# Slot lists of a mixture-of-experts layer: from a one-hot product on TensorE to a table in DRAM

## The chip, the cores and the metric

The kernel runs on one core of one Trainium2 chip. The metric is device time in microseconds (us) of one launch. The engines are TensorE (PE), VectorE (DVE), ScalarE (ACT), GpSimd (POOL) and SyncE (SP); each has its own queue of instructions, and they meet only at semaphores. DMAs are issued from the queues of SP, ACT and POOL.

## The reference, cut to what matters

The program is two transformer blocks on 512 tokens of width 1024. The first block ends in a hierarchical mixture of experts: each token chooses one of 4 groups and in it 2 of 8 experts, so there are 1024 pairs of token and expert over 32 experts.

```
g_sel = argmax(g_logits); top_vals, top_idx = top_k(e_in, 2)
weights = g_w[:, None] * softmax(top_vals)
eid = (g_sel[:, None] * 8 + top_idx).reshape(-1)
# sort the pairs by expert, pad each expert's list, run each block of rows through its expert
hid = silu(xb @ w_gate[e]) * (xb @ w_up[e]);  y = hid @ w_down[e]
y = sum(y_buf[dest].reshape(T, 2, D) * weights[..., None], axis=1)
```

Everything else (a mixer of mLSTM and differential attention ahead of it; a second block with pooling, windowed attention and a 4096 wide feed-forward behind it) is not touched by the change.

## The kernel before, in words

**Stages.** The first mixer runs first, then the routing, then a loop over the 32 experts, then the second block. All weights come through `ring`, six slots of 2 MB, filled by SP. The loop of an expert uses three of them (gate, up, down).

**The routing.** DVE computes the two one-hot choices of each token. A product on TensorE ("rank") counts, for each pair, how many earlier pairs go to the same expert. From it DVE writes `tab` (the number of the first block of each expert, and how many extra blocks it has) and `dest`: for each of the two choices k of each token the slot it gets, counting in blocks of 64 slots. 57 blocks are held.

**The slot lists.** The loop needs the inverse: for each block the list of the 64 tokens in it (`ids[:, block, 0]`) and the 64 rows of the results (`ids[:, block, 1]`, which is token + 512 k). An empty slot holds 1024, which is out of bounds, so that its row is skipped. Before the change DVE splits `dest` into position and block (`slot_at`), makes one-hot tables of both (`POS1H`, `BLK1H`), multiplies one with the row number minus 1024 (`BLKV`), and eight accumulating matmuls on PE ("slots", L600) bring each row number to its place; five small DVE instructions turn that into `idx[:, 0]` (the list of block 0) and `ids`. All of this is on the chip.

**The loop.** For each block POOL copies a column of `ids` to `idx` (`pick`, L1063), gathers 64 rows of `h_rows` from DRAM with an indirect DMA (`gather_rows`, L1067) and scatters the results of the block before with another (`scatter_results`, L1073). PE transposes the rows (`turn_rows`, L608), ACT and DVE split them into a high and a low part (XTS, L1284 and L1737), and PE multiplies (gate and up at L619, down at L646 and L653). The weights are split too: ACT writes the high half (`weights_hi`, L1280), DVE the rest (`weights_lo`, L1732), each in two halves for each of the three units (0 gate, 1 up, 2 down). While expert e runs, ACT and DVE split the weights of e + 1.

**What sets the order.** Nothing is planned: each engine runs its instructions in the order in which they are written. SP loads the weights of experts 0 and 1 as slots of the first stage come free. The load of expert e + 2 waits until the product that reads the raw weights of expert e is done (`freed`, L950, and the DMA at L957).

**Ahead of the loop.** POOL waits for `h_out` (the rows are in DRAM) and `tab_ready`, then for `idx_kept[0]`, and issues the gather of block 0. ACT splits the weights of expert 0; for unit 2 it waits for the "slots" product, since `HI[2]` lies over the routing tables. DVE runs `weights_lo` of unit 0, then `rows_lo(0)`, then units 1 and 2.

Of the kernel before, what the change touches and what calls it, by code (L numbers as in the profile page):

```python
# [26 lines left out]
P = 128  # L27
# [20 lines left out]
BLOCKS_HELD = BLOCKS_MAX + PER_EXPERT_MAX + 1  # L48
NO_ROW = 2 * T
# [13 lines left out]
N_CONSTS2 = 24  # L63
N_SMALL = 17
N_CONSTS = 15
# [28 lines left out]
def build(nc, A, out):  # L94
# [8 lines left out]
    with ctx:  # L103
# [33 lines left out]
        slot_at = sb("slot_at", [P, 2, 2, TT], I32)  # L137
# [29 lines left out]
        IOS, ROWV = m(10112, BLK).bitcast(I32), m(10176, 2 * TT)  # L167
        POS1H, BLK1H, BLKV = m(10240, 2 * TT, BLK), m(10752, 2 * TT, BLOCKS_HELD), m(11264, 2 * TT, BLOCKS_HELD)
        ROWF, HALF2 = m(15360, BLOCKS_HELD)[0:BLK], m(15424, BLOCKS_HELD)[0:BLK]
# [89 lines left out]
        slots_hot = sem("slots_hot")  # L259
        idx_kept = [sem(f"idx_kept{k}") for k in range(2)]  # L260
        waits_met = sem("waits_met")
        ids_ready = sem("ids_ready")
# [22 lines left out]
        consts2 = sem("consts2")  # L285
        pool_step = sem("pool_step")
# [119 lines left out]
        def _(pe):  # L406
# [451 lines left out]
        def _(sp):  # L858
# [73 lines left out]
            sp.dma_start(sink[:, :], A["attn_sinks_2"].to_broadcast([P, W2_HEADS])).then_inc(sink_in, 16)  # L932

# [44 lines left out]
        def _(pool):  # L978
# [9 lines left out]
            def select(t, pattern, base, mult, op, fill, wait=False):  # L988
# [12 lines left out]
            const(pool.iota(inv16[:, :], [[1, 16]], base=1, channel_multiplier=0,  # L1001
                            allow_small_or_imprecise_dtypes=True), True)
# [7 lines left out]
            def roots(names, width):  # L1010
                for nm in names:
# [24 lines left out]
            pool.iota(IOS, [[1, BLK]], base=0, channel_multiplier=0).then_inc(consts2, 1)  # L1036
            pool.iota(ROWV, [[P, 2 * TT]], base=-NO_ROW, channel_multiplier=1,
                      allow_small_or_imprecise_dtypes=True).then_inc(consts2, 1)
            pool.memset(SUM2, 0.0).then_inc(consts2, 1)
            pool.wait_ge(consts2, 10)  # L1040
            for k in range(-1, 2):
                pool.affine_select(out=SUM2, in_=SUM2, pattern=[[-1, 2 * BLK]], base=k * BLK, channel_multiplier=1,
                                   compare_op=ALU.not_equal, fill=1.0).then_inc(consts2, 1)
                pool.wait_ge(consts2, 12 + k)
# [5 lines left out]
            pool.wait_ge(consts2, 14 + W2_HEADS)  # L1050
            pool.affine_select(out=BM, in_=BM, pattern=[[0, W2_HEADS], [-1, 2 * P]], base=P, channel_multiplier=1,
                               compare_op=ALU.is_ge, fill=NEG).then_inc(consts2, 1)
            pool.wait_ge(consts2, 15 + W2_HEADS)
# [3 lines left out]

            pool.wait_ge(h_out, 16 * TT)
# [31 lines left out]

            pool.wait_ge(idx_kept[0], 1)
            gather_rows()
            pool.wait_ge(ids_ready, 1)
# [37 lines left out]
        def _(act):  # L1131
# [47 lines left out]
            act.wait_ge(row_dve, 2)  # L1179
            act.activation(REM, RM, ACT.Exp, scale=-1.0).then_inc(row_act, 1)  # L1180
# [228 lines left out]
        def _(vec):  # L1409
# [251 lines left out]
            vec.wait_ge(consts2, 14)  # L1661
# [52 lines left out]
            step(vec.tensor_scalar(slot_at[:, 1, :, :], dest[:, :, :], BLK.bit_length() - 1, None, ALU.logical_shift_right))  # L1714
            pos, blk = (slot_at[:, a, :, :].rearrange("p k t -> p (k t)").unsqueeze(2) for a in range(2))
            step(vec.tensor_tensor(POS1H, over(pos, 2 * TT, BLK), over(IOS.unsqueeze(1), 2 * TT, BLK), ALU.is_equal))
            step(vec.tensor_tensor(BLK1H, over(blk, 2 * TT, BLOCKS_HELD),
                                   over(IOS[:, 0:BLOCKS_HELD].unsqueeze(1), 2 * TT, BLOCKS_HELD), ALU.is_equal))
            vec.tensor_tensor(BLKV, BLK1H, over(ROWV.unsqueeze(2), 2 * TT, BLOCKS_HELD), ALU.mult).then_inc(slots_hot, 1)
            leave(vec.tensor_scalar(ROWF, filled(vec, "slots")[0:BLK, 0:BLOCKS_HELD], float(NO_ROW), None, ALU.add), "slots")  # L1720
            left(vec, "slots")
            step(vec.tensor_scalar(HALF2, ROWF, float(T), -float(T), ALU.is_ge, ALU.mult))
            vec.tensor_tensor(idx[:, 0, :], ROWF[:, 0:1], HALF2[:, 0:1], ALU.add).then_inc(idx_kept[0], 1)
            step(vec.tensor_copy(ids[:, :, 1], ROWF))
            vec.tensor_tensor(ids[:, :, 0], ROWF, HALF2, ALU.add).then_inc(ids_ready, 1)
# [30 lines left out]
            for half_ in range(2):  # L1756
                weights_lo(0, 0, 0, half_)
            rows_lo(0)
            for u in range(1, 3):
                for half_ in range(2):  # L1760
                    weights_lo(0, u, 0, half_)
            each_expert(vec, block_vec)
# [149 lines left out]
```

## Time and profile before

| What | Value |
|---|---|
| median of 3 runs | 1673.29 us (1669.67 to 1675.77) |
| the profiled execution's own time | 1673.29 us |
| its span, first to last instruction | 1671.3 us |
| PE busy | 1488.6 us (89%) |
| DVE busy | 924.7 us (55%) |
| ACT busy | 733.1 us (44%) |
| POOL busy | 243.7 us (15%) |
| mean granted TensorE clock | 0.910 |

A share of busy time is a mean over stages. The routing and the first blocks of the loop lie at about 400 to 470 us of the span, the loop of the experts at about 438 to 990 us. Times within the span count from its start. PEld is the weight load of TensorE. "issue" is time in which an engine waited for nothing that the profile shows. An engine's name with a q (POOLq, SPq) is its queue: the issuing of a DMA or a register instruction. For a DMA issued from POOL the trace has an instruction (DMA_INDIRECT) whose duration is POOL's own part in it; the data land later.

### The profile page before, as it was taken

The page shows a single profiled execution, that of the slowest core. Times are in us where ns is not written, and L with a number is a line of the kernel's source. Part 1 is how long each engine was busy: PE and PEld are TensorE (multiplying, and loading weights), DVE is VectorE, ACT ScalarE, POOL GpSimd, SP SyncE. Part 2 cuts the span into 40 slices and gives each one's busy share as a digit, 9 for nine tenths or more (in the row PEclk, how much of TensorE's full clock was granted, in tenths as well). Part 3 has the DMA queues.
Part 4 walks back from the last instruction along what each step waited for, and adds up shares of the span by engine and source line. Part 5 has one row for each costly group of instructions (what it writes and reads, how often), then busy time and mean ns, then how long its engine had stood idle before and what let it go on. Part 6 is the DMA issues. An engine that isn't in the chain of part 4 may idle for free.

```text
span 1671.3 us, 19199 instructions
## 1 busy us (share of the span) xinstructions
PE 1488.6 (89%) x6529; PEld 1084.4 (65%) x6530; DVE 924.7 (55%) x1050; ACT 733.1 (44%) x847; POOL 243.7 (15%) x247
## 2 busy tenths in 40 slices
PE   7899988788499999999999968989699999969968
PEld 6788754435367676767676754544388788858746
DVE  6833144413688898889888852462644224421543
ACT  4333232201388888888888841341123213321120
POOL 1011000013222322232222210140000000000030
PEclk8999867788599999999999988979799999979979
DMA  5222420033199999999999986200012222222201
GB/s 203 67 85 101 165 87 1 0 93 126 53 366 385 387 387 387 388 387 385 386 383 382 379 270 181 100 4 23 0 51 101 101 101 101 101 101 96 80 7 44
DMA packets 135235, 294.35 MB, mean 176 GB/s; under 512 B 17870, under 2 KB 19980, under 8 KB 135180
## 3 DMA queue, kind: packets, MB, share of 16 engines
q1 hardware_dynamic: 122732, 270.61, 44.7%
q10 hardware_dynamic: 7168, 14.59, 2.4%
q0 software_dynamic: 5280, 8.40, 1.6%
q8 instruction: 37, 0.61, 0.2%
q14 instruction: 18, 0.15, 0.0%
HBM read 289.64 MB, written 12.85 MB: 181 GB/s over the span
## 4 chain that ended last, share of the span: by engine, by line
PE 64%; DVE 15%; issue 9%; ACT 5%; DMA 4%; DVEq 2%; POOL 1%; SPq 0%; ACTq 0%; POOLq 0%
PE ps L794 11%; PE ps L815 10%; PE ps L457 7%; DVE ring_r L1732 7%; PE ps L619 5%; PE ps L569 3%; PE ps L768 3%; PE ps L653 3%; PE ps L847 3%; PE ps L646 2%; DMA ring<-in_w_gate 2%; PE ps L412 2%; ACT hi L1280 2%; PE ps L501 2%; PE ps L675 2%
## 5 line engine op out<-in xcount | busy, mean ns | idle before, releaser
L1732 DVE TENSOR_TENSOR ring_r<-ring,hi 128x2048 fp32r<-128x2048 f32 x192 | 427.0, 2286 | 45.5 <-ACT hi L1280 45.5
L1280 ACT ACTIVATE hi<-ring 128x2048 fp32r<-128x2048 f32 x192 | 356.5, 1908 | 4.8 <-PE ps L600 2.5
L1459 DVE TENSOR_TENSOR ring_r<-ring,ring_r 128x4096 fp32r<-128x4096 f32 x25 | 110.6, 4425 | 173.8 <-ACT ring_r L1151 173.8
L815 PE MATMUL ps<-ring_r,ats 128*128 128x512 f32 x768 | 179.0, 396 | 4.0 <-DVE ats L1862 3.2
L815 PEld LDWEIGHTS ps<-ring_r,ats 128*128 128x128 f32 x768 | 147.2, 192 | 35.9 <-issue 4.8
L1151 ACT ACTIVATE ring_r<-ring 128x4096 fp32r<-128x4096 f32 x25 | 90.5, 3620 | 167.2 <-PE ps L815 133.7
L1014 POOL TENSOR_TENSOR rsv<-msv,half 128x1 f32<-128x1 f32 (+2 forms) x32 | 32.8, 1027 | 839.1 <-DVE msv L1419 839.1
L619 PE MATMUL ps<-ring_r,XTS 128*128 128x512 f32 x512 | 129.4, 395 | 1.8 <-DVE XTS L1737 1.8
L619 PE MATMUL ps<-hi,XTS 128*128 128x512 f32 x512 | 127.5, 391 | 0.0
L653 PE MATMUL ps<-hi,HIDS 128*64 128x512 f32 x512 | 126.4, 400 | 0.0
L794 PE MATMUL ps<-ring_r,ring_r 128*128 128x512 f32 x512 | 123.1, 393 | 1.8 <-DVE hi L1850 1.8
L457 PE MATMUL ps<-ring_r,ring_r 128*128 128x512 f32 x448 | 111.3, 402 | 5.2 <-DVE M L1484 4.5
L619 PEld LDWEIGHTS ps<-ring_r,XTS 128*128 128x128 f32 x512 | 97.1, 190 | 25.2 <-issue 2.0
L794 PEld LDWEIGHTS ps<-ring_r,ring_r 128*128 128x128 f32 x512 | 97.3, 190 | 22.6 <-issue 2.2
L619 PEld LDWEIGHTS ps<-hi,XTS 128*128 128x128 f32 x512 | 96.9, 189 | 20.4
L653 PEld LDWEIGHTS ps<-hi,HIDS 128*64 128x64 f32 x512 | 71.5, 140 | 53.1 <-issue 7.4
L457 PEld LDWEIGHTS ps<-ring_r,ring_r 128*128 128x128 f32 x448 | 85.9, 194 | 23.8 <-DVE M L1484 4.9
L646 PE MATMUL ps<-ring_r,HIDS 128*64 128x512 f32 x256 | 79.1, 461 | 22.3 <-ACT HIDS L1299 22.3
L1073 POOL DMA_INDIRECT results<-M,idx x33 | 54.5, 1651 | 133.2 <-ACT M L1308 132.9
L1067 POOL DMA_INDIRECT M<-h_rows,idx x33 | 66.0, 1999 | 49.2 <-POOL idx L1063 27.3
L646 PEld LDWEIGHTS ps<-ring_r,HIDS 128*64 128x64 f32 x256 | 36.9, 154 | 49.7 <-issue 36.1
L1063 POOL COPY idx<-M 64x1 int32 x64 | 34.3, 537 | 237.2 <-DMA results<-M,idx 166.7
(295 smaller groups left out, 1943.9 us busy)
## 6 DMA issues: line engine op xcount, KB each, us to landing
ring<-in_w_gate SPq DMA_DIRECT2D x32, 2048.0 KB, 14.2
ring<-in_w_up SPq DMA_DIRECT2D x32, 2048.0 KB
ring<-in_w_down SPq DMA_DIRECT2D x32, 2048.0 KB, 14.7
ring<-in_w_ff SPq DMA_DIRECT2D x16, 2048.0 KB, 8.0
ring<-in_w_in SPq DMA_DIRECT2D x8, 2048.0 KB, 8.4
X<-in_x ACTq DMA_DIRECT2D x8, 512.0 KB, 5.2
ring<-in_w_out SPq DMA_DIRECT2D x2, 2048.0 KB
M<-results ACTq DMA_DIRECT2D x8, 512.0 KB, 7.4
```

Of the source, the lines that this page charges most:

```text
L457: ins = pe.matmul(o, a, b, start=(i == 0 and k == 0), stop=(i == 2 and k == DT - 1))
L619: ins = pe.matmul(ps[:, u, :], XTS[:, k, :, :].rearrange("p s b -> p (s b)"), w[:, k, :], start=(part == 1 and k == 0), stop=(part == 0 an ...
L646: ins = pe.matmul(ps[0:BLK, 4 + c, :], HIDS[:, 0, f, :], w_rest[:, f, c * 512:(c + 1) * 512], start=(f == 0), stop=False)
L653: ins = pe.matmul(ps[0:BLK, 4 + c, :], HIDS[:, a, f, :], w_top[:, f, c * 512:(c + 1) * 512], start=False, stop=(a == 1 and f == FT - 1))
L794: ins = pe.matmul(o, w[a][:, k, f * P:(f + 1) * P], HTS[b][:, k, :], start=(i == 0 and k == 0), stop=(i == 2 and k == DT - 1))
L815: ins = pe.matmul(ps[:, 2 * t + c, :], ATS[a][:, 4 * (n % 4) + k, t * P:(t + 1) * P], w[b][:, k, c * 512:(c + 1) * 512], start=(n % 4 == 0 ...
L1067: pool.indirect_dma_start(out=XG, out_offset=None, in_=h_rows, in_offset=bass.IndirectOffsetOnAxis(idx[:, 0, 0:1], 0), bounds_check=T - 1, ...
L1073: pool.indirect_dma_start(out=results, out_offset=bass.IndirectOffsetOnAxis(idx[:, 1, 0:1], 0), in_=YB.rearrange("p c n -> p (c n)"), in_o ...
L1151: act.activation(split_hi[j % 2][:, :], ring[:, s, :], ACT.Copy).then_inc(s_hi, 1)
L1280: act.activation(HI[u][:, c], ring[:, s, c], ACT.Copy).then_inc(w_hi, 1)
L1459: vec.tensor_tensor(ring_r[s][:, :], ring[:, s, :], split_hi[j % 2][:, :].bitcast(F32), ALU.subtract).then_inc(s_lo, 1)
L1732: vec.tensor_tensor(ring_r[s][:, c], ring[:, s, c], HI[u][:, c].bitcast(F32), ALU.subtract).then_inc(w_lo, 1)
```

## The change

The slot lists are made through a table in DRAM, `slot_tokens` (57 x 64 slots of two 32-bit numbers). POOL fills a tile (`unheld`) with 1024 at the program's start, and SP writes it to the table, between its small loads and its first load of weights. Two iotas for each choice k write `tokid`: the token, and token + 512 k. When `dest` is ready, POOL issues eight indirect DMAs (one for each k and tile of 128 tokens), each of which scatters 128 entries of 8 bytes to the slots named in `dest`, waits for all of them, loads the whole table back into `ids` with a plain DMA of its own queue, waits for that, picks the list of block 0, and gathers. The "slots" product and the ten DVE instructions around it go. ACT's wait for "slots" becomes one for `dest_ready`. DVE splits the weights of units 0 and 1 ahead of `rows_lo(0)` instead of unit 0 alone.

```
+        slot_tokens = nc.dram_tensor("slot_tokens", [SLOTS, 2], I32, kind="Internal").ap()
-            pe.wait_ge(slots_hot, 1)
-            o = open_turn(pe, "slots", 7)
-            for j in range(2 * TT):
-                ins = pe.matmul(o[0:BLK, 0:BLOCKS_HELD], POS1H[:, j, :], BLKV[:, j, :], start=(j == 0), stop=(j == 2 * TT - 1))
-            fill_turn(ins, "slots")
...
+            sp.wait_ge(consts, N_CONSTS)
+            sp.dma_start(slot_tokens.rearrange("(p n) o -> p (n o)", p=BLK),
+                          unheld[:, :, :].rearrange("p n o -> p (n o)")).then_inc(table_in, 16)
...
+            const(pool.memset(unheld[:, :, :], NO_ROW))
+            for k in range(2):
+                const(pool.iota(tokid[:, k, :, 0], [[P, TT]], base=0, channel_multiplier=1))
+                const(pool.iota(tokid[:, k, :, 1], [[P, TT]], base=k * T, channel_multiplier=1), k == 1)
...
+            pool.wait_ge(table_in, 16)
+            pool.wait_ge(dest_ready, 1)
+            for k in range(2):
+                for t in range(TT):
+                    pool.indirect_dma_start(
+                        out=slot_tokens, out_offset=bass.IndirectOffsetOnAxis(dest[:, k, t:t + 1], 0),
+                        in_=tokid[:, k, t, :], in_offset=None).then_inc(ids_out, 16)
+            pool.wait_ge(ids_out, 16 * 2 * TT)
             pool.wait_ge(h_out, 16 * TT)
             pool.wait_ge(tab_ready, 1)
...
+            pool.dma_start(ids, slot_tokens.rearrange("(n p) o -> p n o", p=BLK)).then_inc(idx_in, 16)
+            pool.wait_ge(idx_in, 16)
+            pick(0, 0)
             pool.wait_ge(idx_kept[0], 1)
             gather_rows()
-            pool.wait_ge(ids_ready, 1)
...
                 if u == 2:
-                    filled(act, "slots")
+                    act.wait_ge(dest_ready, 1)
...
-            step(vec.tensor_copy(dest[:, :, :], RS[:, 6:8, :]))
-            step(vec.tensor_scalar(slot_at[:, 0, :, :], dest[:, :, :], BLK - 1, None, ALU.bitwise_and))
...
+            vec.tensor_copy(dest[:, :, :], RS[:, 6:8, :]).then_inc(dest_ready, 1)
```

POOL's queue at the end of the routing, before the change: L1054 is the last of the tables for the second block, L1067 the gather of block 0, and behind it the loop begins.

```order
L1049 TENSOR_SCALAR M<-M 128x256 x8
L1051 AFFINE_SELECT M<-M 128x2048 [waits consts2]
L1054 AFFINE_SELECT M<-M 128x2048 [waits consts2]
L1067 DMA M<-h_rows,idx 64x1024 [waits idx_kept0,tab_ready,h_out]
L379 UNCONDITIONAL_BRANCH [waits ids_ready]
```

The same place of the changed kernel (its line numbers are its own: L1063 the scatter into the table, L1100 the load of the table, L1072 the pick, L1076 the gather).

```order
L1050 TENSOR_SCALAR M<-M 128x256 x8
L1052 AFFINE_SELECT M<-M 128x2048 [waits consts2]
L1055 AFFINE_SELECT M<-M 128x2048 [waits consts2]
L1063 DMA slot_tokens<-tokid,dest 3648x2 [waits dest_ready,table_in]
L1063 DMA slot_tokens<-tokid,dest 3648x2 x7
L1100 DMA M<-slot_tokens 64x57x2 [waits tab_ready,h_out,ids_out]
L1072 COPY idx<-M 64x1 [waits idx_in]
L1076 DMA M<-h_rows,idx 64x1024 [waits idx_kept0]
```

Ahead of the first gather stand nine DMAs and a copy that were not there.

DVE's queue from `dest` to the loop, before the change (ring_r_52, 53 and 54 are the raw weights of units 0, 1 and 2 of expert 0).

```order
L1712 CAST dest<-M 128x8
L1713 TENSOR_SCALAR slot_at<-dest 128x8
L1714 TENSOR_SCALAR slot_at<-dest 128x8
L1716 TENSOR_TENSOR M<-slot_at,M 128x512
L1717 TENSOR_TENSOR M<-slot_at,M 128x456
L1719 TENSOR_TENSOR M<-M 128x456
L1720 TENSOR_SCALAR M<-ps 64x57
...
L1732 TENSOR_TENSOR ring_r_52<-ring,hi_57 128x2048 x2
L1737 TENSOR_TENSOR XTS<-ps,XTS 128x8x64
L1732 TENSOR_TENSOR ring_r_53<-ring,hi_58 128x2048 x2
L1732 TENSOR_TENSOR ring_r_54<-ring,hi_59 128x2048 x2
```

And in the changed kernel, where L1731 is `weights_lo` and L1736 `rows_lo`.

```order
L1723 TENSOR_REDUCE M<-M 128x4
L1724 CAST dest<-M 128x8
L1731 TENSOR_TENSOR ring_r_52<-ring,hi_57 128x2048 x2
L1731 TENSOR_TENSOR ring_r_53<-ring,hi_58 128x2048 x2
L1736 TENSOR_TENSOR XTS<-ps,XTS 128x8x64
L1731 TENSOR_TENSOR ring_r_54<-ring,hi_59 128x2048 x2
```

Ten instructions behind `dest` are gone, and two of the four splits that stood behind the rows (XTS) stand ahead of them.

## Rows read from the trace of the kernel before

**Rows 1.** Busy time and granted clock of stretches around the routing and the loop
```profile
core 0: us, PE busy (x) PEld busy (x) DVE busy (x) ACT busy (x) POOL busy (x), PEclk, DMA share, GB/s
427.00:438.30 11.30, 2.28 (x28) 1.99 (x24) 8.31 (x30) 8.82 (x6) 0.00 (x0) 0.50 0.00 0
438.30:448.80 10.50, 1.09 (x8) 0.95 (x9) 4.84 (x4) 3.80 (x4) 5.49 (x3) 0.50 0.05 14
467.40:883.00 415.60, 397.13 (x1985) 297.35 (x1984) 367.20 (x225) 351.67 (x325) 115.38 (x100) 0.96 1.04 385
```

**Rows 2.** Chain that ended last, routing to first product: start us, us, what
```profile
432.00 0.18 DVE dest L1712
...
434.70 1.97 PE ps L600 x16
...
437.16 0.16 DVE idx L1723
...
438.32 7.35 DMA M<-h_rows,idx
445.66 0.25 issue
...
447.72 0.70 DVE XTS L1737
...
448.81 1.62 PE ps L619 x3
```

**Rows 3.** POOL in order of time, three stretches: start us, us, line, instruction
```profile
438.32 4.85 POOL L1067 DMA_INDIRECT M<-h_rows,idx  x1 [21.98 <-DVE M L1725]
447.28 0.18 POOL L1063 COPY idx<-M 64x1 int32 x1 [4.11 <-PE ps L608]
448.35 0.98 POOL L1067 DMA_INDIRECT M<-h_rows,idx  x1 [0.89 <-POOL idx L1063]
449.63 1.85 POOL L1073 DMA_INDIRECT results<-M,idx  x1 [0.30 <-issue]
...
565.39 0.96 POOL L1067 DMA_INDIRECT M<-h_rows,idx  x1 [0.85 <-POOL idx L1063]
571.06 2.08 POOL L1073 DMA_INDIRECT results<-M,idx  x1 [4.70 <-ACT M L1308]
...
582.15 3.03 POOL L1067 DMA_INDIRECT M<-h_rows,idx  x1 [0.85 <-POOL idx L1063]
```

**Rows 4.** DVE in order of time, beside those of POOL
```profile
437.59 4.48 DVE L1732 TENSOR_TENSOR ring_r<-ring,hi 128x2048 fp32r<-128x2048 f32 x2
...
565.65 13.30 DVE L1732 TENSOR_TENSOR ring_r<-ring,hi 128x2048 fp32r<-128x2048 f32 x6 [1.11 <-ACT hi L1280]
...
582.05 8.90 DVE L1732 TENSOR_TENSOR ring_r<-ring,hi 128x2048 fp32r<-128x2048 f32 x4 [1.11 <-ACT hi L1280]
```

**Rows 5.** ACT in order of time, ahead of the loop
```profile
426.92 7.29 ACT L1280 ACTIVATE hi<-ring 128x2048 fp32r<-128x2048 f32 x4
```

**Rows 6.** SP's queue in order of time: last load before, first in the loop
```profile
398.90 0.37 SPq L945 DMA_DIRECT2D ring<-in_w_up  x1
452.75 0.40 SPq L957 DMA_DIRECT2D ring<-in_w_gate  x1
```

**Rows 7.** Chain that ended last, late in the loop
```profile
889.69 19.67 DMA ring<-in_w_gate
```

**Rows 8.** DMAs of the scatter L1073, issue to landing
```profile
DMA to landing us min/median/max: 2.9/6.9/8.1
```

**Rows 9.** DMA queue from 7 to 9 us: packets, MB, share of 16 engines
```profile
q1 hardware_dynamic: 1160, 0.06, 41.9%
```

**Rows 10.** The program's start in order of time: SP, ACT, POOL
```profile
7.09 0.35 SPq L932 DMA_DIRECT2D sink<-in_attn_sinks  x1
...
25.51 1.06 ACT L1162 ACTIVATE ring_r<-HT 128x1024 fp32r<-128x1024 f32 x1 [2.36 <-PE ps L430]
...
6.40 0.56 POOL L1014 TENSOR_TENSOR rsv<-msv,half 128x1 f32<-128x1 f32 x1 [2.39 <-DVE msv L1419]
```

More of the change, by code:

```diff
@@ L48 @@
 BLOCKS_HELD = BLOCKS_MAX + PER_EXPERT_MAX + 1
+SLOTS = BLOCKS_HELD * BLK
 NO_ROW = 2 * T
@@ L62 @@
 N_PARAMS = 64
-N_CONSTS2 = 24
+N_CONSTS2 = 22
 N_SMALL = 17
-N_CONSTS = 15
+N_CONSTS = 20
 UNITS_1 = ["mq", "mk", "mo", "aq", "ak", "av", "mv", "out0", "out1"]
@@ L136, in build @@
         dest = sb("dest", [P, 2, TT], I32)
-        slot_at = sb("slot_at", [P, 2, 2, TT], I32)
+        tokid = sb("tokid", [P, 2, TT, 2], I32)
         tab = sb("tab", [1, 2, NE + 1], I32)
@@ L166, in build @@
         LAMP = m(13632, 2 * QK)[0:1]
[L167 to L169 removed]
+        unheld = m(17408, 2 * BLOCKS_HELD)[0:BLK].bitcast(I32).rearrange("p (n o) -> p n o", o=2)
         QKM = X[:, :, :].rearrange("p t d -> p (t d)").rearrange("p (c t) -> p c t", c=8)
@@ L258, in build @@
         tab_ready = sem("tab_ready")
-        slots_hot = sem("slots_hot")
+        ids_out = sem("ids_out")
+        table_in = sem("table_in")
         idx_kept = [sem(f"idx_kept{k}") for k in range(2)]
         waits_met = sem("waits_met")
-        ids_ready = sem("ids_ready")
+        idx_in = sem("idx_in")
         rows_in = sem("rows_in")
@@ L285, in build @@
         consts2 = sem("consts2")
+        dest_ready = sem("dest_ready")
         pool_step = sem("pool_step")
@@ L1043, in _ @@
                                    compare_op=ALU.not_equal, fill=1.0).then_inc(consts2, 1)
-                pool.wait_ge(consts2, 12 + k)
+                pool.wait_ge(consts2, 10 + k)
             pool.affine_select(out=UPPER, in_=UPPER, pattern=[[1, P]], base=0, channel_multiplier=-1,
@@ L1049, in _ @@
                 pool.tensor_scalar(BM[:, h, :], DISTI, -(2.0 ** -(h + 1)), None, ALU.mult).then_inc(consts2, 1)
-            pool.wait_ge(consts2, 14 + W2_HEADS)
+            pool.wait_ge(consts2, 12 + W2_HEADS)
             pool.affine_select(out=BM, in_=BM, pattern=[[0, W2_HEADS], [-1, 2 * P]], base=P, channel_multiplier=1,
                                compare_op=ALU.is_ge, fill=NEG).then_inc(consts2, 1)
-            pool.wait_ge(consts2, 15 + W2_HEADS)
+            pool.wait_ge(consts2, 13 + W2_HEADS)
             pool.affine_select(out=BM, in_=BM, pattern=[[0, W2_HEADS], [1, 2 * P]], base=-1, channel_multiplier=-1,
                                compare_op=ALU.is_ge, fill=NEG).then_inc(consts2, 1)
+            pool.wait_ge(table_in, 16)
[6 more added lines that the diff above has]
+            pool.wait_ge(ids_out, 16 * 2 * TT)
             pool.wait_ge(h_out, 16 * TT)
@@ L1179, in _ @@
             act.wait_ge(row_dve, 2)
+            act.wait_ge(table_in, 16)
             act.activation(REM, RM, ACT.Exp, scale=-1.0).then_inc(row_act, 1)
@@ L1660, in _ @@
             left(vec, "route")
-            vec.wait_ge(consts2, 14)
+            vec.wait_ge(consts2, 12)
             step(vec.tensor_reduce(RS[:, 0, :], LG[:, :, 0:NG], AX, ALU.max))
@@ L1711, in _ @@
                 step(vec.tensor_reduce(RS[:, 6 + k, :], o, AX, ALU.add))
-            step(vec.tensor_copy(dest[:, :, :], RS[:, 6:8, :]))
-            step(vec.tensor_scalar(slot_at[:, 0, :, :], dest[:, :, :], BLK - 1, None, ALU.bitwise_and))
[L1714 to L1725, printed above, removed]
+            vec.tensor_copy(dest[:, :, :], RS[:, 6:8, :]).then_inc(dest_ready, 1)
             def weights_lo(e, u, odd, half_):
@@ L1754, in block_vec @@
                             weights_lo(e + 1, u, 1 - odd, half_)
[L1756 to L1759, printed above, removed]
+            for u in range(2):
                 for half_ in range(2):
                     weights_lo(0, u, 0, half_)
+            rows_lo(0)
+            for half_ in range(2):
+                weights_lo(0, 2, 0, half_)
             each_expert(vec, block_vec)
```

7 lines of the change are left out of this document (2 added, 5 removed).

## The prediction

> **What bounds the kernel now.** I read the stretches first, then the chain that ended last, then each engine in order of time where the change lies. Between the routing and the loop of the experts no engine is full: from 427.0 to 448.8 us PE is busy 2.28 and 1.09 us out of 21.8, at a granted clock of 0.50 [rows 1]. The chain there is a string of short steps that wait for one another [rows 2]: DVE writes `dest` (ends at 432.18), five more DVE steps, the "slots" product of 1.97 us, three more DVE steps up to `idx` (ends at 437.32), POOL's gather of block 0 (issued at 438.32, landed 7.35 us later, at 445.67), the transposes, the split of the rows, and the first product at 448.81. Whatever comes later there makes the loop start later.
>
> Inside the loop the engines and the DMAs are both near their limit (PE 397 of 415.6 us, DVE 367, DMA share 1.04 [rows 1]), and near its end the chain lies on the loads of the weights [rows 7]. So the first question is whether the loads could run on while the rows are late. They can't: the last load ahead of the loop is issued at 398.90, the next at 452.75, when the first raw product of expert 0 is done [rows 6]. That is what `freed` asks for. The stream of loads hangs on the start of the loop just as PE does, and nothing in the loop is tied to an event outside it. A start that is later by x makes the end later by x, whether loads or engines bound it.
>
> **The change part by part.** The chain from `dest` to the rows in SBUF is the whole matter. Before, it takes 445.67 - 432.18 = 13.5 us: 5.1 us to `idx` (the removed part: ten DVE instructions, of which eight stand ahead of `idx`, and one product), 1.0 us until POOL's gather starts, 7.35 us of gather [rows 2, 3].
>
> New, in the same time of the span:
>
> (a) `dest` at 432.18, the first scatter starts 1.0 us later, as the gather did behind `idx`: 433.2.
>
> (b) The first scatter. The first indirect DMA of the kernel costs POOL 4.85 us, the second gather 0.98 [rows 3]. I give the first scatter the 4.85: 438.0.
>
> (c) The second. ACT's high parts of units 0 and 1 are there from 434.2 (4 pieces from 426.92 [rows 5]; the first lies ready at 432), so DVE now runs four splits in a row behind `dest`, 2 x 4.48 us [rows 4], until about 441.2. Beside such a run POOL's DMAs take longer: the gather that starts at 582.15, 0.1 us after a run began, takes 3.03 us, the scatter at 571.06 inside a run 2.08, the gather at 565.39, just ahead of one, 0.96 [rows 3, 4]. With 0.30 us between two DMAs that wait for nothing [rows 3] and 2.6 us for it: 440.9.
>
> (d) Six more, DVE being done with its two units and waiting for the rows. A gather of 64 rows costs POOL 0.96 us; 128 entries cost between that and twice that. I take 1.2, near the row, since the first part of such an instruction need not grow with the rows: 6 x (1.2 + 0.30) = 9.0, so 449.9.
>
> (e) Landing of the last. The first gather landed 7.35 - 4.85 = 2.5 us after POOL's part: 452.4.
>
> (f) The plain load behind the wait. From a released semaphore to the start of a DMA on POOL: 0.9 us [rows 3]: 453.3.
>
> (g) POOL's part in it. `ids` is read as 64 x 57 pieces of 8 bytes, 3648 pieces. No row shows a DMA of many pieces from POOL. Below, it costs as much as one of 64 pieces, 0.96 us; above, 57 times 0.96, 55 us, if all of that time grew with the pieces. I take 12 us, 3.3 ns for a piece, between a fifth and a quarter of the 15 ns per row that the upper bound has: part of 0.96 us must be fixed, and a plain load reads no indices. This is the weakest number of the sum.
>
> (h) Moving the pieces. 1160 packets, nearly all of 32 bytes, took 41.9% of 16 engines over 2 us [rows 9], 11.6 ns of one engine each. 3648 are 2.6 us on 16 engines. They run while POOL makes the next, so only the landing stays, 2.5 us as in (e): 467.8.
>
> (i) The pick: 0.25 us to the waiter [rows 2], 0.18 us of copy, 0.87 us until the gather [rows 3]: 469.1.
>
> (j) The gather, no longer the first indirect DMA and with DVE idle: 0.96 + 2.5: 472.6.
>
> The rows come 472.6 - 445.7 = 27 us later.
>
> The rest I cost at nothing. SP's write of the table ahead of the weights adds one DMA, about 0.35 us as that of the sinks; the first weights are then 0.35 us late, and ACT, which splits them, later sits idle for 2.36 us until PE is done with the gates [rows 10]. SP's wait for the constants is met: POOL's constants have 2.39 us of slack ahead of its first root at 6.40 [rows 10] for a memset and four iotas, and SP comes to it at 7.4. ACT splits unit 2 from 434.2 instead of 436.7; nothing waits for it. DVE has 4.5 us less to do behind the rows, but the first product at 448.81 follows XTS, in both orders the first thing DVE does when the rows are there, and the low part of unit 0 is long done. PE's first products run from a clock of 0.50 in any case, since it is there already [rows 1], so a longer idle stretch costs no more than the stretch itself. POOL's clearing of two iotas less lies far ahead.
>
> The sum is against the profiled execution's own time, 1673.29 us (span 1671.3), which is also the median of the runs: 1673.3 + 27 = 1700 us.
>
> **Two rules of the Trainium skill.** For (g) the traces have no row. The Trainium skill, DMA: Bandwidth & Descriptors, section "Anatomy of one DMA — SWDGE (gpsimd) path", says of the making of descriptors in software that many can be emitted before their cost shows. By that, as an estimate, (g) would be about 1 us and the end about 1689 us; no run here shows it.
>
> Rows 3 and 4 show POOL's DMAs at 2 to 3 us beside DVE's splits and at 0.96 without. The Trainium skill, SBUF — State Buffer, section "SBUF: two separate sides", has it that DVE and GpSimd lock each other out of a shared port for a whole instruction, and that descriptors made by GpSimd starve. Here the trace agrees, with a scatter at 2.08 in the middle of a run of 2.2 us pieces. It speaks against the new place of unit 1's splits: they now run beside the scatters. It is in the sum with 1.6 us, in (c).
>
> **The rivals.**
>
> Cheap descriptors: (g) costs about 1 us, for whatever reason. Then 11 us less: 1689. For it: gathers that run alone take 0.96 and 0.98 us [rows 3], as a fixed cost would. Against it: 57 times as many pieces, where even 1 ns for each is 3.6 us. If the first scatter is also as short as the second gather (4 us less) and all eight go at 0.96 + 0.30, 433.2 + 10.1 = 443.0 less the last gap; with 2 us to land (the shortest scatter of the kernel took 2.9 us from issue to landing, POOL's part in it [rows 8]), 0.9, 0.96, 2.5, 1.3 and 3.5 us the rows are there at 454: 8.5 us late, 1682. That is the lowest sum that the rows allow.
>
> Dear descriptors: (g) goes with the pieces, 27 us (half of 0.96 grows with them) to 55 us. The sum is 1715 to 1743. For it: each piece needs its own read and write wherever the list is made, and no row excludes it; scatters that land late (up to 8.1 us under the loop's load [rows 8]) would add to it. Against it: nothing else moves while these DMAs do, the DMA share there is 0.05 [rows 1].
>
> The other side, not slower: the first block catches up. DVE's four splits and ACT's unit 2 are done ahead, so the first expert could end earlier than now, and the splits of expert 1 with it. It decides only if the delay is under 5 us, and the most it could give is the 4.5 us of DVE that are gone from behind the rows; DVE waits for ACT in the loop, 1.11 us ahead of a run [rows 4]. With the lowest delay of 8.5 us the best would be 4 us slower: 1677. To be faster, the whole trip through DRAM, two landings of 2 us at least and ten instructions of POOL, would have to fit into the 5.1 us that are removed.
>
> That the change doesn't do what it says: the table could be ready before it is needed, if the scatters were hidden under other work. `dest` is the last result of the routing and the gather the next step, so nothing lies between them.
>
> **How the numbers follow.** Delay of 20 to 36 us, as forecast: 0.52, 1693 to 1709. Cheap descriptors, 8.5 to 20 us: 0.28. Dear ones, above 36 us: 0.17. Not slower or hardly: 0.03. The range that holds 8 in 10 leaves out the lowest and the upper end: 1684 to 1727. A measurement of this kernel tells about 0.3%, 5 us, from no change. Slower by more: 0.97; within: 0.02; faster: 0.01.
>
> **What would show it.** In the changed kernel's trace: nothing on POOL between 416 and 433 us, then eight scatters, the first long, the next beside DVE's splits, the others shorter; the load at about 453 with a POOL part of several us; the rows at about 473 instead of 445.7; PE's first product about 27 us later, and the same distance to the end: the loop's length (first product to the last) unchanged within 2 us, and so the part after it. SP's next load would come 27 us later than 452.75. The forecast is wrong if POOL's part in the load is under 2 us or over 22, if the first scatter isn't the long one, if the loop gets shorter behind the later start, or if the stretch before 427 us moves by more than 0.5 us.

## The result, and the profile after

The changed kernel takes 1685.96 us (median of 5 runs, 1683.94 to 1688.34), the kernel before, timed with it, 1672.85 us (5 runs, 1669.67 to 1675.77). The ratio is 1.008 [1.006, 1.0099]: 13.1 us slower. The profiled run took 1685.04 us (span 1683.3), 11.75 more than that of before. The forecast was 27 us, 1700 us in all, with a range of 1684 to 1727; the measured time lies at the lower end of that range. The likeliest case began at 20 us, and what came is the rival that the prediction called "cheap descriptors", 8.5 to 20 us, to which it had given 0.28.

POOL in order of time in the changed kernel: start us, us, line, instruction, and in brackets how long POOL was idle before it and what ended that.

```profile
432.41 2.44 POOL L1063 DMA_INDIRECT slot_tokens<-tokid,dest  x1 [16.75 <-DVE dest L1724]
435.15 1.60 POOL L1063 DMA_INDIRECT slot_tokens<-tokid,dest  x1 [0.30 <-issue]
437.06 1.89 POOL L1063 DMA_INDIRECT slot_tokens<-tokid,dest  x1 [0.30 <-issue]
439.26 1.90 POOL L1063 DMA_INDIRECT slot_tokens<-tokid,dest  x1 [0.30 <-issue]
...
445.25 0.96 POOL L1063 DMA_INDIRECT slot_tokens<-tokid,dest  x1 [0.30 <-issue]
447.63 1.63 POOL L1100 DMA_DIRECT2D M<-slot_tokens  x1 [1.43 <-DMA slot_tokens<-tokid,dest]
453.23 0.18 POOL L1072 COPY idx<-M 64x1 int32<-64x1 int32 x1 [3.97 <-DMA M<-slot_tokens]
454.24 1.02 POOL L1076 DMA_INDIRECT M<-h_rows,idx  x1 [0.82 <-POOL idx L1072]
```

These are the nine DMAs and the copy ahead of the first gather, where before there was one gather [rows 3]. The load of 3648 pieces costs POOL 1.63 us. The first four scatters are longer than the last four, which all take 0.96 (three are left out).

DVE and SP in order of time beside them.

```profile
431.43 8.89 DVE L1731 TENSOR_TENSOR ring_r<-ring,hi 128x2048 fp32r<-128x2048 f32 x4
460.04 0.69 DVE L1736 TENSOR_TENSOR XTS<-ps,XTS 128x512 fp32r<-128x512 f32 x1 [19.72 <-ACT XTS L1296]
464.72 0.39 SPq L957 DMA_DIRECT2D ring<-in_w_gate  x1
```

DVE's four splits run back to back from `dest` to 440.32, and the four scatters that start before that are the long ones. SP's next load, at 452.75 before [rows 6], comes 11.97 us later.

The chain that ended last, from `dest` to the first product: start us, us, what.

```profile
431.35 0.18 DVE dest L1724
431.57 0.84 issue
432.41 2.44 POOL slot_tokens L1063
...
445.25 2.10 DMA slot_tokens<-tokid,dest
447.35 0.29 issue
447.63 5.54 DMA M<-slot_tokens
...
454.24 3.74 DMA M<-h_rows,idx
...
461.12 8.88 PE ps L616 x32
```

It answers to rows 2: `dest` ends at 431.52 (before 432.17), the gather of 3.74 us lands at 457.98 (445.67), the first product starts at 461.12 (448.81). From `dest` to the first product it was 16.64 us, now 29.60: 12.96 us more. Of the load's 5.54 us only 1.63 are POOL's part; 3.91 go by until it has landed.

Stretches of the changed kernel: us, busy time of PE, PEld, DVE, ACT and POOL with instructions, granted clock, DMA share, GB/s. The second has the length of that in rows 1, 12.3 us later.

```profile
427.00:450.00 23.00, 0.00 (x0) 0.00 (x0) 12.80 (x20) 10.15 (x6) 13.30 (x9) 0.50 0.01 0
479.70:895.30 415.60, 396.53 (x1987) 296.93 (x1986) 368.17 (x225) 352.83 (x323) 118.79 (x100) 0.97 1.04 386
```

PE does nothing at all while the table is made, at a granted clock of 0.50 as before (the lower of its two levels, 1.2 GHz), and the DMAs move next to nothing (share 0.01). The loop is the same work at the same pace. From the first product to the end of the span it is 1222.18 us; before, 1222.49. So the profiled 11.75 us are 12.96 of delay, less 0.65 that the stretch up to `dest` was shorter in this execution, less 0.31 behind the first product, less 0.25 around the span.

### The profile page after: what moved, and what is told of

It reads as the page before. It is cut to its first block, busy times and chain, and to the rows that moved or that the text cites. A ratio compares the mean times of both kernels' runs of the same rounds, so it can differ in the third digit from the quotient of the medians.

```text
span 1683.3 us, 19172 instructions
## 1 busy us (share of the span) xinstructions
PE 1481.1 (88%) x6513; PEld 1078.9 (64%) x6514; DVE 921.3 (55%) x1040; ACT 733.0 (44%) x847; POOL 250.4 (15%) x260
## 4 chain that ended last, share of the span: by engine, by line
PE 63%; DVE 16%; issue 9%; ACT 5%; DMA 3%; DVEq 2%; POOL 1%; SPq 0%; ACTq 0%; POOLq 0%
PE ps L791 10%; PE ps L812 10%; PE ps L459 7%; DVE ring_r L1731 7%; PE ps L616 6%; PE ps L571 3%; PE ps L765 3%; PE ps L844 3%; PE ps L650 3%; PE ps L414 2%; PE ps L643 2%; ACT hi L1292 2%; PE ps L503 2%; PE ps L672 2%; PE ps L538 1%
## 5 line engine op out<-in xcount | busy, mean ns | idle before, releaser
L1731 DVE TENSOR_TENSOR ring_r<-ring,hi 128x2048 fp32r<-128x2048 f32 x192 | 427.0, 2287 | 53.7 <-ACT hi L1292 53.5
L1072 POOL COPY idx<-M 64x1 int32 (+1 forms) x65 | 34.3, 528 | 249.4 <-DMA results<-M,idx 165.1
L624 PEld LDWEIGHTS ps<-M 128*128 128x128 f32 x512 | 64.4, 191 | 5.0 <-issue 1.0
```

The costliest lines, as they stand in the source:

```text
L624: ins = pe.matmul(ps[:, 2 + u, f * BLK:(f + 1) * BLK], GUS[:, u, f * P:(f + 1) * P], SUM2[:, 0:BLK], start=True, stop=True)
L1731: vec.tensor_tensor(ring_r[s][:, c], ring[:, s, c], HI[u][:, c].bitcast(F32), ALU.subtract).then_inc(w_lo, 1)
```

## The experiments

Below, D is the distance from the end of `dest` to the start of the first product, read in each run's trace (before 16.64, changed 29.60 us), "the rest" is from there to the span's end. Ratios are to the kernel before in the same comparison.

**Is a delay all there is?** The kernel before, with twelve clearings (`DELAYS` is 12) of the gather's target ahead of the first gather.

```diff
             pool.wait_ge(idx_kept[0], 1)
+            for n in range(DELAYS):
+                pool.memset(XG, 0.0).then_inc(delayed, 1)
+                pool.wait_ge(delayed, n + 1)
             gather_rows()
```

> The kernel before, with nothing added but 12 clearings of the tile XG on POOL between idx and the first gather, each waited for (0.95 us each in the trace, about 1.05 with the wait): the rows come 12.6 us later. Theory A (a later start is a later end, and the change cost 13 us because the round trip is 12 to 13 us long and not 27): the end is 11 to 14 us later, 1684 to 1687. Theory B (the loop takes up part of a late start, and the round trip costs more elsewhere): the first product is 12.6 us late and the end under 9 us, below 1682.

```profile
439.10 11.96 POOL L1095 MEMSET M<- 64x1024 f32 x12 [21.13 <-DVE idx L1728]
451.97 1.23 POOL L1069 DMA_INDIRECT M<-h_rows,idx  x1 [0.92 <-POOL M L1095]
```

Ratio 1.0044 [1.0029, 1.0059], +7.4 us, less than expected and, as a number, what Theory B forecast. But by Theory B the first product is 12.6 us late and the part behind it shorter, and neither is so. The trace (POOL in order of time, above) says why: the clearings take 11.96 us, but the gather itself costs POOL 1.23 us instead of 4.85 [rows 3], so D is 25.22, 8.6 more and not 12. DVE's two splits had ended at 443.7, long before this gather. The rest is 1224.16, 1.7 longer than in the first trace of before, not shorter. The delay passes on, and most of the 4.85 us of the first gather turns out not to be a matter of being first. The clearings themselves took 0.94 us each, the four that started beside DVE's splits like the other eight.

**What a scatter costs.** The changed kernel with eight more scatters, into a second table that nobody reads, ahead of the eight.

```diff
-            for k in range(2):
-                for t in range(TT):
+            for tbl, k, t in [(tbl, k, t) for tbl in (spare_table, slot_tokens) for k in range(2) for t in range(TT)]:
                     pool.indirect_dma_start(
-                        out=slot_tokens,
+                        out=tbl,
...
-            pool.wait_ge(ids_out, 16 * 2 * TT)
+            pool.wait_ge(ids_out, 16 * 4 * TT)
```

> The changed kernel with sixteen scatters instead of eight: the first eight go to a spare table that nobody reads. Theory A: each of the eight more costs POOL 0.96 us and 0.30 between two, fixed and not by entries, since DVE's four splits still cover only the first four: 8 x 1.26 = 10.1 us, 1696. If the cost of the first scatters came from the first use of the instruction and not from DVE, the same; if a landing queues behind eight more writes of 128 entries, 1 to 2 us on top. Theory B: the end moves by 5 to 8 us only.

```profile
443.80 0.95 POOL L1063 DMA_INDIRECT spare_table<-tokid,dest  x1 [0.30 <-issue]
...
457.68 0.96 POOL L1063 DMA_INDIRECT slot_tokens<-tokid,dest  x1 [0.30 <-issue]
```

Ratio 1.0133 [1.0116, 1.0151], 1696.91 us against an expected 1696. D is 39.47, 9.87 more than in the changed kernel: 8 x (0.96 + 0.30) = 10.1. In POOL's rows only the first four scatters are long, as in the changed kernel; all twelve behind them take 0.96. This settles that the scatters are on the path, each with 1.26 us.

**Who makes the first scatters long: DVE's order.** The changed kernel with DVE's order of before (only unit 0 split ahead of the rows).

```diff
-            for u in range(2):
-                for half_ in range(2):
-                    weights_lo(0, u, 0, half_)
+            for half_ in range(2):
+                weights_lo(0, 0, 0, half_)
             rows_lo(0)
-            for half_ in range(2):
-                weights_lo(0, 2, 0, half_)
+            for u in range(1, 3):
+                for half_ in range(2):
+                    weights_lo(0, u, 0, half_)
```

> The changed kernel with DVE's old order: unit 1's splits again behind the rows, so two splits stand beside the scatters instead of four. If each scatter waits for the end of the DVE instruction beside it (as 1.60, 1.89 and 1.90 us of POOL's part suggest), the third and fourth take 0.96 us: 1.9 us sooner to the rows, and the first product 1.9 us sooner. The time: 1684, if the first expert doesn't need the splits; if its 1 to 2.5 us of catching up came from them, they are given back and the time stays at 1686.

POOL and DVE in order of time:

```profile
433.71 2.44 POOL L1063 DMA_INDIRECT slot_tokens<-tokid,dest  x1 [16.75 <-DVE dest L1724]
436.45 1.60 POOL L1063 DMA_INDIRECT slot_tokens<-tokid,dest  x1 [0.30 <-issue]
438.35 0.96 POOL L1063 DMA_INDIRECT slot_tokens<-tokid,dest  x1 [0.30 <-issue]
...
432.73 4.49 DVE L1731 TENSOR_TENSOR ring_r<-ring,hi 128x2048 fp32r<-128x2048 f32 x2
```

With two splits, two scatters are long; with four, four. D falls by 1.68 us (2 x 0.94 would be 1.9; the load of the table took 0.24 longer in this execution). The ratio, 1.0075 [1.0059, 1.0091], can't be told from the changed kernel's: the effect shows in the trace and is too small for the times to tell.

**The kernel before once more**, unchanged, for a second trace.

> The kernel before once more, for its trace: how much the loop's length (first product to the load of the results, 545.5 us in the first trace, 549.9 in that of the changed kernel) moves from one execution to the next. If the 4.4 us are of the change, it is 545 to 546 again; if not, it lies anywhere between 544 and 550.

It took 1675.35 us (one run). POOL's row:

```profile
440.35 4.85 POOL L1067 DMA_INDIRECT M<-h_rows,idx  x1 [22.00 <-DVE M L1725]
```

The same 4.85, with D 16.79 and the rest 1222.41: two traces of one kernel agree within 0.15 us in both. From the first product to the load of the results (the fourth of ACT's) it is 545.25 us here, 545.53 in the first trace, 549.94 in that of the changed kernel: the 4.4 us are no chance between executions of one kernel. Over all traces of this study they go with DVE's order. The six with the old order lie between 545.25 and 547.08, the changed kernel with the old order (545.35) among them; of the seven with the new order six lie between 547.93 and 550.36, and the seventh, the last experiment below, where the splits start later, at 545.08. The part behind that load is 676.99 to 678.79 us in the kernels built on the one before and 671.50 to 676.79 in those built on the changed one. What makes the one longer and the other shorter no run here shows.

**The load by rows instead of by pieces.** The table lies so that each partition reads one run of 456 bytes; the place of a slot then needs three more DVE steps on `dest`.

```diff
-            vec.tensor_copy(dest[:, :, :], RS[:, 6:8, :]).then_inc(dest_ready, 1)
+            step(vec.tensor_copy(dest[:, :, :], RS[:, 6:8, :]))
+            step(vec.tensor_scalar(slot_at[:, 0, :, :], dest[:, :, :], BLK - 1, None, ALU.bitwise_and))
+            step(vec.tensor_scalar(slot_at[:, 1, :, :], dest[:, :, :], BLK.bit_length() - 1, None, ALU.logical_shift_right))
+            vec.scalar_tensor_tensor(out=dest[:, :, :], in0=slot_at[:, 0, :, :], scalar=float(BLOCKS_HELD), in1=slot_at[:, 1, :, :],
+                                     op0=ALU.mult, op1=ALU.add).then_inc(dest_ready, 1)
...
-            pool.dma_start(ids, slot_tokens.rearrange("(n p) o -> p n o", p=BLK)).then_inc(idx_in, 16)
+            pool.dma_start(ids.rearrange("p n o -> p (n o)"), slot_tokens.rearrange("(p n) o -> p (n o)", p=BLK)).then_inc(idx_in, 16)
```

> The changed kernel with the table laid out by position, so that the load reads one run of 456 bytes for each of 64 partitions (64 pieces, not 3648). DVE makes the slot number in three more steps (0.6 us). Theory A1 (the load's 5.5 us grow with the pieces: POOL's part 1.6 us against 0.96, and 11.6 ns for each piece on 16 engines, 2.6 us): the load lands 2.2 to 2.7 us after its issue, the rows come 2.4 us sooner than in the changed kernel, 1683. Theory A2 (the 5.5 us are a fixed cost of reading DRAM and of the completion): the load takes 5 us still, and the rows come 0.1 to 0.6 us later than in the changed kernel.

POOL's row of the load and the chain's:

```profile
449.15 0.60 POOL L1101 DMA_DIRECT2D M<-slot_tokens  x1 [1.43 <-DMA slot_tokens<-tokid,dest]
...
449.15 1.94 DMA M<-slot_tokens
```

Ratio 1.0054 [1.0035, 1.0073]. 64 pieces cost POOL 0.60 us and land in 1.94; 3648 cost 1.63 and land in 5.54. Between these two points a piece costs POOL (1.63 - 0.60) / 3584 = 0.29 ns, less than a tenth of the 3.3 ns that I had taken, and the pieces' larger price, 3.60 - 1.03 = 2.57 us, lies behind POOL's part, in moving and landing them. From the end of the first step on `dest` the first product comes 3.4 us sooner than in the changed kernel (2.4 expected): 3.60 from the load and 0.44 from a gather that landed sooner, less 0.61 for the three steps. The time, 1683.59 us, is the 1683 of Theory A1.

**Only block 0's entries first**, then the gather, then the whole table behind it.

```diff
-            pool.dma_start(ids, slot_tokens.rearrange("(n p) o -> p n o", p=BLK)).then_inc(idx_in, 16)
+            pool.dma_start(idx[:, 0, :], slot_tokens[0:BLK, 0:1], allow_slow_non_contiguous=True).then_inc(idx_in, 16)
             pool.wait_ge(idx_in, 16)
-            pick(0, 0)
-            pool.wait_ge(idx_kept[0], 1)
+            pool.sem_inc(idx_kept[0], 1)
             gather_rows()
+            pool.dma_start(ids, slot_tokens.rearrange("(n p) o -> p n o", p=BLK)).then_inc(idx_in, 16)
+            pool.wait_ge(idx_in, 32)
```

> The changed kernel with the list of block 0 loaded alone, straight into idx (64 pieces of 4 bytes); the pick goes, the gather follows, and the whole table is loaded behind the gather. By A1 the small load takes 2.2 to 2.7 us and the rows come 3.3 us sooner; by A2 5 us, and the rows come 1 us sooner (the pick and what stands around it). The load of the whole table, now behind the gather, ends about 2 us after PE has transposed the rows, which nothing waits for. Time by A1 1682, by A2 1685.

POOL in order of time, and the chain's row of the small load:

```profile
447.90 0.60 POOL L1100 DMA_DIRECT2D idx<-slot_tokens  x1 [1.43 <-DMA slot_tokens<-tokid,dest]
450.76 1.01 POOL L1076 DMA_INDIRECT M<-h_rows,idx  x1 [2.26 <-DMA idx<-slot_tokens]
451.77 1.63 POOL L1104 DMA_DIRECT2D M<-slot_tokens  x1
...
447.90 1.96 DMA idx<-slot_tokens
```

D falls by 3.98 us, the ratio is 1.0057 [1.0037, 1.0077]. The time, 1683.98 us, lies between the two forecasts and can't tell them apart; the trace does. The small load costs what that of whole rows did (0.60 and 1.96), as by A1, the large one its 1.63 again, now behind the gather. But something does wait for the large load: POOL picks the list of block 1 only behind it, 1.99 us after the first product instead of 1.53 us ahead of it, and the rows of block 1 (DVE's XTS) come 13.1 us behind the first product instead of 12.2.

**The table loaded by ACT.** ACT waits for the scatters and issues the load ahead of its part of the rows; POOL's load and its wait for the scatters go.

```diff
+            act.wait_ge(ids_out, 16 * 2 * TT)
+            act.dma_start(ids, slot_tokens.rearrange("(n p) o -> p n o", p=BLK)).then_inc(idx_in, 16)
             rows_hi(0)
```

> The changed kernel with the whole table loaded from ACT's queue instead of POOL's. If the 12 us that I gave to POOL's making of 3648 pieces are anywhere, they show as a difference: ACT's load of as many pieces would be far shorter than POOL's. If POOL's part is cheap (1.63 us in the trace), the load lands 4 to 5.5 us after ACT's issue and the rows move by under 1 us either way: 1684 to 1686.

ACT's row, the chain's, and the DMA queues from 448 to 454 us (packets, MB, share of 16 engines):

```profile
448.99 0.67 ACTq L1332 DMA_DIRECT2D M<-slot_tokens  x1
...
448.99 4.43 DMA M<-slot_tokens
...
q10 hardware_dynamic: 3664, 0.03, 33.7%
```

The same stretch of the changed kernel:

```profile
q0 software_dynamic: 80, 0.03, 18.0%
```

With POOL out of it the load still takes 4.43 us. D falls by 1.56 (under 1 was expected), the ratio is 1.0053 [1.0035, 1.0071]. In ACT's queue the 3648 pieces are 3664 packets, which keep the DMA engines busy for 0.337 x 6 us x 16 = 32 us in all, 8.8 ns each; in POOL's they are 80 packets and 17 us. Which of the two queues issues the load matters less (5.54 against 4.43 us) than that it has 3648 pieces and not 64 (1.94).

**The changed kernel once more**, in the same comparison.

> The changed kernel once more, for its trace: whether PE's stall of 4.1 us at expert 30, for which the profile names no waiter and behind which the clock is at 0.5 for 6 us, is there again. It was in two of two traces with DVE's new order and in none of four with the old one. If it belongs to the order of DVE, it is in this trace and in those of the other three kernels of this call; if it is chance, it is missing from at least one.

1683.62 us, D 29.54, the rest 1223.16. Its trace, and the others, bear on a detail behind the first product. PE's first two groups of products take less than before, 3.41 and 2.00 us (before 3.75 and 2.98): the granted clock is 0.56 and 1.00 in them (before 0.50 and 0.63), and the fourteenth load of the loop comes 73.7 us behind the first product instead of 76.1. This gain is not of the change alone: the delayed kernel, which has nothing of it, has that load at 73.6. Late in the loop PE stands still for some time. Its row there, of the changed kernel:

```profile
970.36 3.75 PE L616 MATMUL ps<-ring_r,XTS 128*128 128x512 f32 x8 [4.06 <-issue]
```

and of this second trace:

```profile
967.08 3.53 PE L616 MATMUL ps<-ring_r,XTS 128*128 128x512 f32 x8 [3.08 <-issue]
```

Neither trace of before has it. If it were DVE's new order alone, every kernel with that order would show it; the one with ACT's load and the last one below have the order and no such row. So the order alone doesn't bring it. But the five traces that have the stall (2.46 to 4.06 us) are all of that order, five of seven, and none of the six with the old order has it, so the order may well be a part of it. The profile names no semaphore for it, and its cause stays open. It doesn't move the sum much: over all 13 traces the rest is between 1218.9 and 1227.1 us.

**No split beside the first gather.** The kernel before, with a tiny write of POOL behind the gather, for which DVE waits ahead of unit 0's splits.

```diff
             gather_rows()
+            pool.memset(mark[:, :], 0.0).then_inc(issued, 1)
...
+            vec.wait_ge(issued, 1)
             for half_ in range(2):
                 weights_lo(0, 0, 0, half_)
             rows_lo(0)
```

> The kernel before, with DVE's first splits held until POOL is through with its part of the first gather (a small memset behind the gather signals it). If the 4.85 us of that part are the first use of the instruction, they stay and the splits come late: 2 us slower, 1675. If they are DVE's two splits beside it (in the run with a pure delay the part was 1.23 us, with the splits long done), it is 1.2 us, the rows land 3.6 us sooner, the splits fit ahead of XTS, and the first product comes 3.5 us sooner: 1670, under the kernel before.

POOL, DVE and PE in order of time:

```profile
437.88 1.23 POOL L1069 DMA_INDIRECT M<-h_rows,idx  x1 [22.01 <-DVE M L1728]
...
439.26 4.50 DVE L1735 TENSOR_TENSOR ring_r<-ring,hi 128x2048 fp32r<-128x2048 f32 x2 [2.03 <-POOL mark L1095]
...
444.75 3.75 PE L621 MATMUL ps<-ring_r,XTS 128*128 128x512 f32 x8 [2.04 <-DVE XTS L1740]
```

1669.56 us, ratio 0.9974 [0.9962, 0.9987] (12 runs): 4 us faster than the kernel before, and the fastest of this study. The gather's part falls from 4.85 to 1.23, D from 16.64 to 13.01. The same gather is still the first indirect DMA of the kernel. POOL's next pick and gather, now beside the splits, take 0.81 and 2.72 us instead of 0.18 and 0.98; the first product doesn't wait for them.

**Only one of the two splits moved away.** The kernel before, with the split of one half of unit 0 moved into the gap in which DVE waits for the "slots" product, and the other left beside the gather.

```diff
                 ... ALU.mult).then_inc(slots_hot, 1)
+            weights_lo(0, 0, 0, 0)
...
-            for half_ in range(2):
-                weights_lo(0, 0, 0, half_)
+            weights_lo(0, 0, 0, 1)
             rows_lo(0)
```

> The kernel before, with the first half of unit 0's split moved into the 2.05 us in which DVE waits for the slots product; the second half stays beside the first gather. idx comes 0.3 us later. One DVE instruction of 2.2 us is left beside the gather, so POOL's part ends with it, about 1 us behind: 2.9 to 3.2 us instead of 4.85. The first product 1.4 us sooner: 1672, which the times alone can't tell from no change.

POOL and DVE in order of time:

```profile
440.61 2.66 POOL L1067 DMA_INDIRECT M<-h_rows,idx  x1 [22.07 <-DVE M L1733]
...
439.88 2.28 DVE L1657 TENSOR_TENSOR ring_r<-ring,hi 128x2048 fp32r<-128x2048 f32 x1
```

The gather ends at 443.27, 1.1 us behind the end of the one split (442.16). D is 14.67, 2.0 less (1.4 expected); the ratio 0.9991 [0.998, 1.0002] tells no change.

**No split beside the scatters.** The changed kernel with the same wait, behind the eighth scatter.

```diff
+            pool.memset(mark[:, :], 0.0).then_inc(issued, 1)
             pool.wait_ge(ids_out, 16 * 2 * TT)
...
+            vec.wait_ge(issued, 1)
             for u in range(2):
                 for half_ in range(2):
                     weights_lo(0, u, 0, half_)
```

> The changed kernel, with DVE's four splits held until POOL is through with its part of the eighth scatter. If the scatters wait for the DVE instruction beside them, all eight take 0.96 us of POOL's part (the first up to 1.25) and the last ends 3.7 to 4.0 us sooner; the splits (8.9 us) fit between it and XTS. The first product comes 3.7 to 4.0 us sooner, the end too: 1681. If the 2.44 us of the first scatter are its first use, it stays, and only 2.5 us are won.

POOL and DVE in order of time:

```profile
432.81 1.27 POOL L1065 DMA_INDIRECT slot_tokens<-tokid,dest  x1 [16.78 <-DVE dest L1727]
434.38 0.97 POOL L1065 DMA_INDIRECT slot_tokens<-tokid,dest  x1 [0.30 <-issue]
...
444.35 1.63 POOL L1103 DMA_DIRECT2D M<-slot_tokens  x1 [1.31 <-DMA slot_tokens<-tokid,dest]
450.07 1.94 POOL L1075 COPY idx<-M 64x1 int32<-64x1 int32 x1 [4.09 <-DMA M<-slot_tokens]
...
443.07 8.90 DVE L1734 TENSOR_TENSOR ring_r<-ring,hi 128x2048 fp32r<-128x2048 f32 x4 [11.15 <-POOL mark L1068]
```

Every scatter is short now, and 4 us were expected of it. But the splits, moved to 443.07 to 451.97, now lie beside the pick, which takes 1.94 us instead of 0.18 and ends at 452.01, with the last split. D falls by 2.08 only; the ratio is 1.0063 [1.004, 1.0087]. The cost had moved to the next instruction of POOL that reads a tile. The load of the table also runs beside the splits, from 444.35 to 445.98, across the end of one of them, and takes 1.63 us as it does with DVE idle: a plain load from DRAM is not held up.

## Why the prediction was wrong in size and right in kind

The direction, the place and the path held: the trip through DRAM lies between `dest` and the first gather, nothing hides it, and the loads, the engines and the end follow the first product. The size was twice too large. By the prediction's steps, forecast against the trace of the changed kernel:

| step | forecast us | measured us |
|---|---|---|
| (a) `dest` to first scatter | 1.0 | 0.88 |
| (b) to (d) eight scatters, POOL's part with gaps | 16.7 | 13.8 |
| (e) landing of the last | 2.5 | 1.14 |
| (f) to the load | 0.9 | 0.28 |
| (g) POOL's part in the load | 12 | 1.63 |
| (h) landing behind it | 2.5 | 3.91 |
| (i) pick, to the gather | 1.3 | 1.06 |
| (j) gather | 3.5 | 3.74 |
| sum, `dest` to the rows | 40.4 | 26.45 |

**The failed step is (g), a term mis-sized by 10.4 us.** I had no row for a plain DMA of many pieces from POOL, had bounds of 0.96 and 55 us, and chose 12 by spreading part of the 0.96 us of an indirect gather over its 64 rows, as if that part grew with the pieces. The loads of 64 and of 3648 pieces show 0.60 us for the first and 0.29 ns for each piece more. My argument against the cheap case, "even 1 ns for each is 3.6 us", assumed the very thing in question: nothing in the rows said that POOL handles pieces one by one. Between bounds 57-fold apart I took a value that no row gave; the nearest row was the lower bound, and the measured 1.63 us lies beside it. With 1.63 in place of 12 the same sum gives 1690 us.

The trace agrees here with what the Trainium skill, DMA: Bandwidth & Descriptors, section "Anatomy of one DMA — SWDGE (gpsimd) path", says of many descriptors costing little to make; the prediction cited it and gave its case 0.28. Its fixed cost of about 2.0 us for a DMA agrees too, with 1.94 and 1.96 us for the loads of 64 pieces. What it adds to that goes by bytes alone, and by that, as an estimate, 29 kB would take 2.1 us; for 29 kB in pieces of 8 bytes it doesn't hold, 5.54 us.

**(b) to (d), 2.9 us too much.** I gave the first scatter the 4.85 us of "the first indirect DMA of the kernel". That was the wrong reason for that row: with DVE quiet the first gather takes 1.23 us, so 3.6 of its 4.85 us were DVE's two splits [rows 4], and being first is worth about 0.3 (1.23 to 1.27 us against 0.96). In the changed kernel a scatter ends 0.8 to 1.2 us behind the end of the split beside it, and the splits end every 2.2 us; that gives 2.44, 1.60, 1.89, 1.90. So four scatters were slowed where I had slowed one. The four took 7.83 us together, where the forecast has 9.85 for them (7.45 for the first two and 1.2 for each of the others): two errors, a first scatter too long and splits beside too few of them, cancelled in part, and that was luck. And 128 entries cost POOL 0.96 us, the same as 64 rows of 4 KB, where I took 1.2.

**(e), (f) and (h).** The scatter lands 1.14 us behind POOL's part and the load starts 0.28 us behind that; I had borrowed 2.5 and 0.9 from a gather of 64 x 4 KB and from a POOL copy. The load's pieces do not move beside POOL's making them, as (h) had it: POOL's part ends at 449.27, the load's packets run from 450.03 to 451.80, and it has landed at 453.18, so that 3.91 us follow POOL's part instead of 2.5.

**What I costed at nothing held in sum, and in part by luck.** The table's first write took SP 0.61 us (0.35 forecast), and no cost of it shows: the stretch up to `dest` was 0.65 us shorter in that execution. I had named a move of more than 0.5 us as a sign of being wrong; over all thirteen traces `dest` ends between 429.20 and 434.40 us, so that bound was tighter than the kernel's own spread. The part behind the first product stayed within 0.31 us as a whole. Its inner split did not: the loop was 4.4 us longer in the changed kernel's trace and the part behind it 4.7 shorter (2.4 and 1.8 in its second trace), against my 2 us for each. I had given DVE's new order no cost, yet the longer loop goes with it; that the part behind it came out shorter by about as much, I had no reason to expect, and its cause is open. In the delayed kernel, with none of the change in it, both parts stayed within 1.6 us of before.

## What to carry to other kernels

A cost without a row should be bounded, and the value taken near the row that is nearest in kind, not scaled by a count that no row shows to matter. Before a long first instance is called a cost of being first, look at what ran beside it: a small delay of the other engine can tell. And where one engine's DMA issues lie on the path, the other engine's long vector instructions belong behind them, which gave 4 us for one wait here (0.26%, with 0.13 to 0.38% as the interval), but only if they don't then land on the next instruction of that path.

## What the runs showed of the hardware

POOL's part in an indirect DMA, and also POOL's small copy, waits for the end of a DVE `tensor_tensor` that reads two float32 tiles and runs beside it: 0.96 us became 1.60 to 1.90, 1.23 became 4.85 beside two splits and 2.66 beside one, and the copy's 0.18 became 1.94. The Trainium skill, SBUF — State Buffer, section "SBUF: two separate sides", describes a lock of this kind for a DVE instruction with two inputs in SBUF against a GpSimd one that reads SBUF; the traces agree, also in what is not held up: POOL's clearings (0.94 us beside a split and without) and the plain load of the table (1.63 us beside a split and without), neither of which reads a tile. The whole loop of the kernel before bears it out: of its 32 gathers behind the first, the 15 that start inside a split take 2.43 to 3.05 us and end 0.83 us behind that split's end, every one, and the 17 others take 0.95 to 0.98. Why the first gather missed the boundary between the two splits (at 439.8) and waited for the second, while each scatter got in at the next boundary, stays open.

A plain load in pieces of 8 bytes costs more in moving and landing than in issuing, whichever queue issues it: 5.54 us from POOL, 4.43 from ACT, 1.94 for the same bytes in 64 rows. The same access became 80 packets from POOL's queue and 3664 from ACT's.
